# Making both halves of a split weight tile on GpSimd, from the fifth tile on

## The reference, cut to what matters

```
h = _rmsnorm(x, norm_gain) @ w_in
u, z_a, q, k, v, z_b, g_a, g_b = jnp.split(h, SPLITS, axis=-1)
br_a = g * sigmoid(g @ w_glu + b_glu) * silu(z_a)       # g = gelu(S5(u))
br_b = o_attn * silu(z_b)
mixed = sigmoid(g_a) * (br_a @ w_out_a) + sigmoid(g_b) * (br_b @ w_out_b)
y = x + mixed @ w_o
```

## Time and profile before

| | us |
|---|---|
| median of 3 runs | 1660.41 |
| lowest and highest | 1659.61, 1661.41 |
| the profiled execution, its time | 1659.57 |
| its span, first to last instruction | 1657.8 |
| TensorE matmul busy | 1595.0 (96%) |
| VectorE busy | 684.0 (41%) |
| ScalarE busy | 463.0 (28%) |
| GpSimd busy | 492.4 (30%) |

### The profile page before, as it was taken

How to read it: one execution, slowest core, us unless ns; L and a number is a source line. 1 busy time by engine, 2 the same in 40 slices (tenths; PEclk the granted TensorE clock), 3 DMA queues, 4 the chain that set the end, 5 groups by cost and what they waited for, 6 DMA issues and landing times.

```text
span 1657.8 us, 26281 instructions
## 1 busy us (share of the span) xinstructions
PE 1595.0 (96%) x10543; PEld 1522.8 (92%) x10543; DVE 684.0 (41%) x1043; ACT 463.0 (28%) x560; POOL 492.4 (30%) x120
## 2 busy tenths in 40 slices
PE   7899986999999799999999999999999999999999
PEld 7899975999999799999999999998999999988887
DVE  8788874771588513213132232324841111520000
ACT  7311221221111133424434244335421111311110
POOL 4322212222333232322323223221533333333332
PEclk9999997999999899999999999999999999999999
DMA  7544339233422344354443554454433333324430
GB/s 259 137 130 138 117 120 144 107 108 125 128 97 92 104 134 119 106 147 114 140 119 106 143 115 135 127 154 144 149 125 124 123 123 123 105 95 140 140 140 32
DMA packets 163412, 208.40 MB, mean 126 GB/s; under 512 B 106482, under 2 KB 123682, under 8 KB 149668
## 3 DMA queue, kind: packets, MB, share of 16 engines
q1 hardware_dynamic: 46740, 125.00, 23.4%
q10 hardware_dynamic: 116624, 82.71, 18.6%
HBM read 162.27 MB, written 42.77 MB: 124 GB/s over the span
## 4 chain that ended last, share of the span: by engine, by line
PE 78%; DVE 13%; issue 4%; ACTq 2%; ACT 1%; DVEq 0%; DMA 0%; SPq 0%
PE ps L438 57%; PE ps L696 13%; DVE rc L1174 3%; DVE pt L1174 2%; DVE H L1174 2%; PE ps L596 1%; ACTq L739 1%; PE ps L610 1%; DVE sq L1182 1%; PE ps L590 1%; DVE sq L1174 1%; PE ps L589 1%; DVE ssum L1165 1%; PE ps L460 1%; DVE powers L1239 1%
## 5 line engine op out<-in xcount | busy, mean ns | idle before, releaser
L405 POOL TENSOR_TENSOR w_lo<-raw,w_hi 128x2048 fp32r<-128x2048 f32 (+1 forms) x111 | 490.4, 4419 | 1140.7 <-ACT w_hi L736 1140.7
L438 PE MATMUL ps<-x_hi,w_hi 128*128 128x320 f32 x2112 | 491.7, 314 | 33.8 <-DVE E L1357 17.8
L438 PE MATMUL ps<-x_lo,w_hi 128*128 128x320 f32 x2112 | 484.7, 311 | 0.0
L438 PE MATMUL ps<-x_hi,w_lo 128*128 128x320 f32 x2112 | 484.1, 311 | 0.0
L736 ACT ACTIVATE w_hi<-raw 128x2048 fp32r<-128x2048 f32 (+1 forms) x111 | 196.7, 1775 | 771.5 <-PE ps L438 414.9
L438 PEld LDWEIGHTS ps<-x_hi,w_hi 128*128 128x128 f32 x2112 | 356.1, 190 | 39.2 <-DVE E L1357 18.8
L438 PEld LDWEIGHTS ps<-x_lo,w_hi 128*128 128x128 f32 x2112 | 356.3, 189 | 0.0
L438 PEld LDWEIGHTS ps<-x_hi,w_lo 128*128 128x128 f32 x2112 | 356.2, 189 | 0.0
L1357 DVE TENSOR_TENSOR E<-ps,rinv 128x640 f32<-128x640 f32 x58 | 47.6, 824 | 343.9 <-PE ps L438 329.2
L736 ACT ACT_TABLE_LOAD x76 | 97.5, 1283 | 115.2 <-issue 89.4
L696 PE MATMUL ps<-w_hi,mix_hi 128*128 128x512 f32 x320 | 124.6, 389 | 0.0
(11 more groups left out here) (200 smaller groups left out, 1704.1 us busy)
## 6 DMA issues: line engine op xcount, KB each, us to landing
raw<-in_wts SPq DMA_DIRECT2D x99, 1024.0 KB, 4.9
g_scr<-E ACTq DMA_DIRECT2D x32, 320.0 KB, 2.2
E<-g_scr ACTq DMA_DIRECT2D x32, 320.0 KB, 3.1
x_raw<-in_xT SPq DMA_DIRECT2D x16, 320.0 KB, 8.0
z_scr<-E ACTq DMA_DIRECT2D x16, 320.0 KB, 2.2
Y<-in_x_tok ACTq DMA_DIRECT2D x20, 256.0 KB, 4.7
out_y_tok<-Y ACTq DMA_DIRECT2D x20, 256.0 KB, 2.6
c_scr<-powers ACTq DMA_DIRECT2D x16, 256.0 KB, 4.0
```

The source lines that it names most:

```text
L405: return nc.gpsimd.tensor_tensor(w_lo[p][:, cols], raw[p][:, cols], w_hi[p][:, cols].bitcast(F32), ALU.subtract)
L438: last = nc.tensor.matmul(outs[:, h, :], w[p][:, c:c + P], act[k][:, h * HALF:(h + 1) * HALF], start=(k == 0 and w is w_hi and act is hi), ...
```

## The change

From tile 4 on, GpSimd makes both halves. Before each subtraction it now waits for the loaded tile and for the buffer to be free, copies `raw[p]` to `w_hi[p]`, waits for that copy (it increments `w_hi_done` itself) and subtracts as before. The conditions of the copy are those of ScalarE's `hi`. Every call of `hi` and the function go from ScalarE's program, 98 copies. The loop over tiles is written out by Python in place of the loop on the engine, 49 turns.

```diff
-            with pool.Fori(2, N_UNITS // 2) as i:
+            for i in range(2, N_UNITS // 2):
                 for p in range(2):
-
+                    pool.wait_ge(w_loaded[p], 16 * i + 16 * p - 16)
+                    pool.wait_ge(proj_done, 2 * i + p - 1)
+                    nc.gpsimd.tensor_copy(w_hi[p][:], raw[p][:]).then_inc(w_hi_done, 1)
                     pool.wait_ge(w_hi_done, 2 * i + p + 1)
                     low(p).then_inc(w_split, 1)
...
-            def hi(n, p, k):
-
-                act.wait_ge(w_loaded[p], 16 * k + 16 * p - 16)
-                act.wait_ge(proj_done, n - 1)
-                A(w_hi[p][:], raw[p][:], ACT.Copy).then_inc(w_hi_done, 1)
-
...
             def store_u(n, p, i):
-                hi(n + 2, p, i + 1)
                 act.wait_ge(acc_free, n + 1)
...
             def squares_q(i):
                 square_q(i, 0)
-                hi(U_Q + 2 * i + 3, 1, U_Q // 2 + i + 1)
                 square_q(i, 1)
...
             def gate(func, scr, n, idx, p, i, split=True):
-                if split:
-                    hi(n + 2, p, i + 1)
                 act.wait_ge(acc_free, n + 1)
...
                     else:
-                        hi(U_GLU + n + 2, n % 2, (U_GLU + n) // 2 + 1)
                         act.wait_ge(proj_done, U_GLU + n + 1)
...
             for n in range(2, 16):
-                hi(U_WO + n, n % 2, (U_WO + n) // 2)
```

More of the change, by code:

```diff
@@ L879, in _ @@
             bt_evac(2)
-            hi(U_V + 2, 1, U_V // 2 + 1)
             ssm_store(2)
@@ L887, in _ @@
             load(v_out, Eb[1][:, PROMPT - P:TOK], v_stored)
-            hi(U_Q + 2, 0, U_Q // 2 + 1)
             store_c(3)
@@ L904, in _ @@
                 square_q(0, p)
-            hi(U_Q + 3, 1, U_Q // 2 + 1)
             ssm_store(3)
@@ L912, in finish_q @@
                 root(Eb[3], 2 * i + 3)
-                hi(U_Q + 2 * i + 4, 0, U_Q // 2 + i + 2)
                 store_q(i, 1)
@@ L1108, in _ @@
                 for p in range(2):
-                    hi(U_OUT + 2 * i + p, p, U_OUT // 2 + i)
                     act.wait_ge(mix_done, 2 * i + p - 1)
@@ L1115, in mix_hi_tile @@
                 A(mix_tiles[0][t], mixed[:, t, :], ACT.Copy).then_inc(mix_hi_done, 1)
-            hi(U_WO, 0, U_WO // 2)
             for t in range(2):
@@ L1126, in _ @@
                 mix_hi_tile(t)
-                if t == 8:
-                    hi(U_WO + 1, 1, U_WO // 2)
             for t in range(TT):
```

## The result

| | before | after |
|---|---|---|
| median us (lowest to highest, runs) | 1660.91 (1659.61 to 1661.88, 4) | 1683.80 (1681.16 to 1686.68, 4) |
| profiled execution: time, span | 1659.57, 1657.8 | 1686.68, 1684.9 |

The change makes the kernel slower: ratio 1.014 [1.0122, 1.0158], +22.9 us in the medians against a forecast of +22.4. The total is right; several of its terms are not, and that they add up so well is in part luck. The two profiled executions lie 27.1 us apart, more than the medians, since the one after is the longest of its four. What follows is an account of those 27.1 us.

What follows compares the result with a forecast made beforehand. GpSimd time added inside the scan, where its work holds VectorE's two-SBUF-input operations, is added to the kernel. Terms 0.2 - 1.2 - 1.9 - 2.8 + 23.6 + 4.5 = +22.4 us gave 1683; range 1658 to 1702, its own 1677 to 1691.

Steps and rivals of the forecast that it cites:

- step 7: Gates, 612 to 1147 us: TensorE is full and VectorE has slack, so the copies add 0.
- The rival of a slow copy: A GpSimd copy takes 2.5 to 4.64 us; c = 3 gives 1697 us, c = 4.64 gives 1720; chance 0.20.
- the one of a copy that leaves VectorE free: Only the subtraction holds VectorE, copies cost nothing: sum -1.9, 1658.5 us, no change; chance 0.11.
- the evacuation that ends the scan: Sign in the trace: it comes near 583 us in place of 563.77, after ten tiles.
- TensorE's waits for VectorE's E: Sign in the trace: TensorE's total wait for VectorE's E goes up by about 25 us.
- the square's wait: Sign in the trace: TensorE's wait for one square on ScalarE, 14.9 us before, comes near 13.
- the state products': Sign in the trace: TensorE's two waits for ScalarE to empty the state products, 3.0 us before, come near 0.2.
- Step 6: The scan: ten copies of 2.0 us less 0.8, plus 4.4 for tile 33's subtraction, add 23.6 us.
- Step 9: From 1165 us to the end: w_split is never late and residual sums read PSUM, so 0.
- Step 4: At 281 us: ScalarE's w_hi goes from between the two squares TensorE waits for, -1.9 us.
- steps 1 to 3: Start to 231 us: +0.2 for 57 to 118, 0 for 118 to 188, -1.2 for 188 to 231.
- Steps 1, 5 and 8: Start (57 to 118 us) +0.2; state products (371 and 392 us) -2.8; GLU's start, tile 67's split before g_lo, +4.5.

Runs made afterwards that it cites:

- the twice-made copies: Changed kernel with GpSimd's copy made twice for tiles 24 to 33 (the scan), same values written again: 1704.53 us, ratio 1.0265.
- the doubled gate copies: Changed kernel with GpSimd's copy made twice for tiles 38 to 65 (the gates): 1681.56 us, ratio 1.013.
- four places: Changed kernel with the copies of tiles 15, 24 to 33, 67 and 87 back on ScalarE, other 85 on GpSimd: 1656.47 us, ratio 0.9979 to before.

## Why the prediction was right, and where it was not

**What held.** The bound was read correctly: busy shares said nothing, and the chain of VectorE's two-input operations in the scan was where GpSimd's time turns into kernel time. The copy holds VectorE, as the twice-made copies show (+17.5 us for ten), and the same copies cost nothing in the gates, as step 7 had it for a stage where TensorE is full. The tenth tile came into the scan in the profiled run. The rival of a slow copy falls with 1.93 us, the one of a copy that leaves VectorE free with the row of 440.13 and with the doubled copies. Of the signs named ahead, the evacuation that ends the scan came at 579.82 (forecast 583), with ten tiles ahead of it. TensorE's waits for VectorE's E grew by 14.8 us and, with 5.4 in w_o, 20.2 (forecast 25); the square's wait was 18.0 (forecast 13) and the state products' 1.3 (forecast 0.2). The Trainium skill's GPSIMD Engine Reference (8, Key points) exempts no GpSimd operation from the contention with two-input VectorE operations; the trace agrees, 1.92 us under the copy.

**Step 6, 23.6 against 16.9: the term was mis-sized.** It charged each copy at its full length, 10 x 2.0 - 0.8 = 19.2, and tile 33's subtraction at 4.4. Summed over the changed scan, the ten copies held VectorE for 14.2 us and the ten subtractions for 41.5, against 38.5 for nine before: 17.2, close to the 16.9 of the whole scan. So the copies cost 14.2 for the 19.2 forecast, and the tenth subtraction 3.0 for 4.4. A copy of 1.9 us costs 1.4, since it begins beside an operation already under way, in a gap between dependent operations, or beside an evacuation from PSUM. The second copy of a pair, which has no such start, costs 1.75. Charging the length of the disturbing instruction, not what is left of it once VectorE reaches a held form, was the error. The tenth tile is also not certain: it fell outside in the run with the doubled gate copies.

**Step 9, 0 against +7.6: this step failed.** It asked whether w_split could be late. It never is: none of TensorE's waits is for w_lo. It did not ask what the split now lands on. The prediction saw that effect for tiles 33 and 67, both kept late by ScalarE's queue, and stopped there; tile 87 was the third. "Residual sums read PSUM" is true, but mix_lo, with two SBUF inputs, stands ahead of them in the queue. Tile 87 moved back gives 7.4 us back.

**Step 4, -1.9 against 0, and the U loads.** Taking the copy from between the squares did nothing, since TensorE's own work on the first square covers it. Further, "SyncE's loads ... come about when they did" was wrong for one load: tile 17's now runs beside ScalarE's eight U loads and their issue takes 3.2 us more. This ate the gain of steps 1 to 3, which was larger than forecast (-3.1 for -1.0). A part of that gain is a wait for kk, the state matrices, before unit 6 that went away, 3.43 us, and with it a stretch at a lower clock. The row from 115 to 124 us, after and then before:

```profile
115.00:124.00 9.00, 8.92 (x66) 8.49 (x64) 7.37 (x19) 3.18 (x5) 3.39 (x1) 1.00 0.55 193
```
```profile
115.00:124.00 9.00, 8.15 (x39) 8.15 (x40) 8.00 (x17) 2.84 (x5) 4.51 (x1) 0.62 0.58 195
```

The mean granted clock was 0.62 over that stretch, in part at the 1.2 GHz level behind the wait, and is now 1.00; units 6 and 7 took 30.1 us and now about 28.2.

**Steps 1, 5 and 8: right in kind.** The wait at the start grew by 3.3 us (forecast 3.6). The state products' waits went from 3.0 to 1.3 us, since the E of their gate still stands before them. The GLU lost 3.4 us (forecast 4.5), and tile 67 moved back gives 3.3.

So the sum fitted since errors cancelled: that is luck, and not a sign that the terms were good. Against the profiled difference: -6.7 in the scan, -1.1 in the GLU, +7.6 in w_o, and +4.8 in all that lies before the scan, together +4.6 of the 4.7 missed. Against the median, 1683.80, they nearly vanish, since two of its four runs are 4.5 and 5.5 us shorter than the profiled one.

## What to carry to other kernels

When work moves to GpSimd, its own time says little; list every place where the moved work will now run and look at what VectorE does there, since a busy queue may have kept an operation late and so out of the way. Charge the part of GpSimd's instruction that VectorE really waits out, about three quarters of 1.9 us here, and only where VectorE's chain ends a stage. Moving the copies everywhere but in four places, 85 of 98, beat both all and none of them.

## What the hardware showed that I had not expected

- A VectorE COPY with one SBUF input is held too. At 572.45 `H<-hs_fin` took 4.60 us beside the subtraction; the same operation, undisturbed in the kernel before, took 0.43. The Trainium skill's DVE page on opcodes (DVE: opcode table, instruction layouts, handler registers and perf-mode slots; 7, Perf-mode slots) says that one-input operations reach a two-port mode even in fp32, and the GPSIMD Engine Reference names that mode as contending; the trace agrees with both.
- The holding goes both ways. With four places moved back, a GpSimd copy took 8.85 us instead of 1.9. VectorE ran eight two-input operations back to back from 1157.51 to 1172.95, and the copy ended 1.7 us behind the last of them. In the kernel before, the subtraction of 1171.18 took 9.69 us beside the same operations. The copy in the kernel with four places:

```profile
1165.77 8.85 POOL L437 CAST w_hi<-raw 128x2048 fp32r<-128x2048 f32 x1 [3.88 <-PE ps L450]
```

- The cast of 128 x 2048 took GpSimd 1.93 us in the mean and ScalarE 1.89 to 1.91, about the same, against 4.73 for the subtraction with its two inputs.
- Issuing eight strided 320 KB loads took a queue 16.9 us, and 20.1 with one 1 MB load of another queue beside them; the last issue alone took 5.84 us instead of 3.14.
